# Rotary embedding of one attention: partner halves by four small SBUF copies in place of a rotation matmul, with TensorE's order rewritten

## The reference

```python
def apply_rope(t, cos, sin):
    tf = t.astype(jnp.float32)
    t1, t2 = tf[..., :HEAD_DIM // 2], tf[..., HEAD_DIM // 2:]
    return jnp.concatenate([t1 * cos - t2 * sin, t2 * cos + t1 * sin], axis=-1).astype(t.dtype)

def odd_mixer(h, w_in, w_out, cos, sin):
    q, k, v = jnp.split(h @ w_in, 3, axis=-1)
    o = moba_attention(apply_rope(to_heads(q, H_MOBA), cos, sin),
                       apply_rope(to_heads(k, H_MOBA), cos, sin),
                       to_heads(v, H_MOBA))
    return from_heads(o) @ w_out
```

## Time and profile before

| | |
|---|---|
| median of 3 runs | 1939.98 us (1939.98 to 1940.36) |
| the profiled execution, its own time | 1937.51 us |
| its span in the profile | 1935.7 us |
| TensorE busy | 1896.3 us, 98% of the span |
| DVE busy | 1391.6 us, 72% |
| ACT busy | 1024.7 us, 53% |
| the eight pairs, first Q to the third output slab | 406.58 to 489.50 us |

### The profile page before, as it was taken

How to read it: one execution, slowest core, us unless ns; L and a number is a source line. 1 busy time by engine, 2 the same in 40 slices (tenths; PEclk the granted TensorE clock), 3 DMA queues, 4 the chain that set the end, 5 groups by cost and what they waited for, 6 DMA issues and landing times.

```text
span 1935.7 us, 32388 instructions
## 1 busy us (share of the span) xinstructions
PE 1896.3 (98%) x11234; PEld 1638.0 (85%) x11234; DVE 1391.6 (72%) x2850; ACT 1024.7 (53%) x1739; POOL 335.9 (17%) x147
## 2 busy tenths in 40 slices
PE   8989999999999999999999999999999999999998
PEld 7867887788788889998899998888898988888886
DVE  6685556667655568898997678976778876666666
ACT  6565455555644466666434556665555553333333
POOL 0000000000000000000000268886666500000000
PEclk9999999999999999999999999999999999999999
DMA  6524655443355544443344445554444455555554
GB/s 222 195 77 134 217 182 173 143 153 120 131 186 187 190 141 156 149 135 110 131 138 165 145 144 183 185 186 152 142 142 142 141 185 194 191 191 193 195 194 153
DMA packets 85581, 314.11 MB, mean 162 GB/s; under 512 B 9504, under 2 KB 9632, under 8 KB 85280
## 3 DMA queue, kind: packets, MB, share of 16 engines
q1 hardware_dynamic: 85472, 312.65, 48.6%
HBM read 311.56 MB, written 1.05 MB: 161 GB/s over the span
## 4 chain that ended last, share of the span: by engine, by line
PE 87%; DVE 8%; ACT 3%; issue 1%; DMA 1%; SPq 0%; DVEq 0%; ACTq 0%
PE ps L416 23%; PE ps L401 13%; PE ps L2625 11%; PE ps L282 11%; PE ps L2629 6%; PE ps L1886 5%; PE ps L2809 3%; PE ps L2442 3%; PE ps L1955 2%; PE ps L788 1%; DVE wsplit L266 1%; PE ps L432 1%; DMA ring<-in_weights 1%; ACT wsplit L260 1%; PE ps L2271 1%
## 5 line engine op out<-in xcount | busy, mean ns | idle before, releaser
L260 ACT ACTIVATE wsplit<-ring 128x1024 fp32r<-128x1024 f32 x572 | 604.6, 1058 | 512.8 <-PE ps L416 266.4
L266 DVE TENSOR_TENSOR wsplit<-ring,wsplit 128x1024 fp32r<-128x1024 f32 x438 | 539.3, 1235 | 304.1 <-ACT wsplit L260 302.8
L416 PE MATMUL ps<-wsplit,gsplit 128*128 128x512 f32 x1992 | 456.5, 390 | 0.0
L266 POOL TENSOR_TENSOR wsplit<-ring,wsplit 128x1024 fp32r<-128x1024 f32 x134 | 321.7, 2402 | 696.3 <-ACT wsplit L260 696.0
L416 PEld LDWEIGHTS ps<-wsplit,gsplit 128*128 128x128 f32 x1992 | 373.2, 188 | 81.3 <-issue 4.0
L2625 PE MATMUL ps<-hsplit,wsplit 128*128 128x512 f32 x1024 | 368.3, 402 | 0.5 <-DVE work L2672 0.5
L401 PE MATMUL ps<-wsplit,hsplit 128*128 128x512 f32 x1248 | 299.7, 395 | 5.6 <-DVE wsplit L266 3.0
L2629 PE MATMUL ps<-hsplit,wsplit 128*128 128x256 f32 x1024 | 286.2, 280 | 0.0
L401 PEld LDWEIGHTS ps<-wsplit,hsplit 128*128 128x128 f32 x1248 | 232.7, 189 | 57.8 <-DVE wsplit L266 6.8
L282 PE MATMUL ps<-hsplit,wsplit 128*128 128x256 f32 x1992 | 258.5, 287 | 7.2 <-DVE hsplit L736 2.1
L282 PEld LDWEIGHTS ps<-hsplit,wsplit 128*128 128x128 f32 x1992 | 243.6, 191 | 17.4 <-issue 9.1
(11 more groups left out here) (325 smaller groups left out, 1945.5 us busy)
## 6 DMA issues: line engine op xcount, KB each, us to landing
ring<-in_weights SPq DMA_DIRECT2D x572, 512.0 KB, 3.3
work<-in_weights SPq DMA_DIRECT2D x8, 512.0 KB, 4.9
work<-in_tables SPq DMA_DIRECT2D x1, 1995.0 KB, 10.4
work<-in_decay SPq DMA_DIRECT2D x2, 512.0 KB, 4.0
work<-in_subkeys SPq DMA_DIRECT2D x2, 512.0 KB, 5.0
out_x<-work SPq DMA_DIRECT2D x2, 512.0 KB, 2.6
...
```

What stands on the lines that cost most here:

```text
L260: act.activation(wsplit[:, n % RING, 0, :], slab(s), ACT.Copy).then_inc(S("split", "lead"), 1)
L266: eng.tensor_tensor(wsplit[:, n % RING, 1, :], slab(s), wsplit[:, n % RING, 0, :], ALU.subtract).then_inc(S("split", RESTS[stream][0]), 1)
L416: mm = pe.matmul(YR[:, tt, half * 512:(half + 1) * 512], gsplit[:, slot, b, tt * P:(tt + 1) * P], wsplit[:, n, a, half * 512:(half + 1) * ...
```

## The change

The matmul with `rot` in this attention is gone. ACT copies query and key out of PSUM one by one, each as soon as its own product is done (`moba_raw_scalar`, L1222 of the changed kernel), waits for that copy, and issues four DMAs of 32 partitions x 256 elements (32 KB) from `qk_raw` to `qk_tmp`, which swap the halves of both heads: eight DMAs for each pair, 64 in all, from ACT's own queue. The sign of the rotation moves into the table `sin`, and `rot` loses its minus sign, since another attention goes on using both with instructions of the same kind and shape. `turn` is now called for query and key apart, with 128x256 operations. The copy for query u waits until both turns of pair u - 1 are done, the copy for key u until the turn of query u is done. TensorE's loop has the order Q(u+1), P(u-1), S(u), K(u+1), V(u-1), and the projections of pair 1 stand ahead of the loop.

```diff
--- before.py
+++ after.py
@@ -1139,18 +1139,24 @@
     def moba_pair(name, u):
         return S("pair", name), MOBA_FROM + u + 1
 
-    def moba_rotate_tensor(pe, st, u):
-        pe.wait_ge(*moba_pair("qk_sb", u))
-        pe.matmul(ps[:, 2, :], table("rot"), qk_raw[:, :, :].rearrange("p a t -> p (a t)"), start=True,
-                  stop=True).then_inc(S(st, "turned"), 1)
+    def moba_half(name, u, a):
+        return S("pair", name), MOBA_FROM + 2 * u + a + 1
 
     def moba_query_tensor(pe, st, u):
         if u:
-            pe.wait_ge(*moba_pair("qk_sb", u - 1))
-        split_project(pe, ps[:, 0, 0:T], st, 8 + 2 * u)
+            pe.wait_ge(*moba_half("qk_sb", u - 1, 0))
+        split_project(pe, ps[:, 0, 0:T], st, 8 + 2 * u).then_inc(S("pair", "qk"), 1)
 
     def moba_key_tensor(pe, st, u):
+        if u:
+            pe.wait_ge(*moba_half("qk_sb", u - 1, 1))
         split_project(pe, ps[:, 1, 0:T], st, 9 + 2 * u).then_inc(S("pair", "qk"), 1)
+
+    def moba_scores_tensor(pe, st, u):
+        pe.wait_ge(S(st, "qk_turn"), 2 * u + 2)
+        if u:
+            pe.wait_ge(*moba_pair("tops", u - 1))
+        scores_tensor(pe, qk_turn[:, 0, :], qk_turn[:, 1, :], 3).then_inc(S("pair", "scores"), 1)
 
     def moba_probs_tensor(pe, u):
         pe.wait_ge(*moba_pair("probs", u))
@@ -1179,26 +1185,21 @@
             mm.then_inc(S(st, "v"), 1)
         moba_query_tensor(pe, st, 0)
         moba_key_tensor(pe, st, 0)
-        moba_rotate_tensor(pe, st, 0)
-        for u in range(8):
-            last = u == 7
-            if not last:
-                moba_query_tensor(pe, st, u + 1)
-            pe.wait_ge(S(st, "qk_turn"), u + 1)
-            if u:
-                pe.wait_ge(*moba_pair("tops", u - 1))
-            scores_tensor(pe, qk_turn[:, 0, :], qk_turn[:, 1, :], 3).then_inc(S("pair", "scores"), 1)
-            if not last:
-                moba_key_tensor(pe, st, u + 1)
-            if u:
-                moba_probs_tensor(pe, u - 1)
-            if not last:
-                moba_rotate_tensor(pe, st, u + 1)
-            if u > 5:
-                pe.wait_ge(*moba_pair("o_low", u - 6))
-                out_tile_tensor(pe, "out1", u - 6, 0, hsplit, u == 6)
-            if u:
-                moba_values_tensor(pe, st, u - 1)
+        moba_query_tensor(pe, st, 1)
+        moba_key_tensor(pe, st, 1)
+        moba_scores_tensor(pe, st, 0)
+        for u in range(1, 7):
+            moba_query_tensor(pe, st, u + 1)
+            moba_probs_tensor(pe, u - 1)
+            moba_scores_tensor(pe, st, u)
+            moba_key_tensor(pe, st, u + 1)
+            moba_values_tensor(pe, st, u - 1)
+        moba_probs_tensor(pe, 6)
+        for c in range(2):
+            pe.wait_ge(*moba_pair("o_low", c))
+            out_tile_tensor(pe, "out1", c, 0, hsplit, c == 0)
+        moba_scores_tensor(pe, st, 7)
+        moba_values_tensor(pe, st, 6)
 
         def out(c):
             out_chunk_tensor(pe, "out1", c, hsplit, moba_pair("o_low", c))
@@ -1218,9 +1219,15 @@
     def moba_rest(v, k):
         rest_of(v, *(("moba", k) if k < N_MOBA else ("out1", k - N_MOBA)))
 
-    def moba_query_key_scalar(act, u):
-        act.wait_ge(*moba_pair("qk", u))
-        act.activation(qk_raw[:, :, :], ps[:, 0:2, 0:T], ACT.Copy).then_inc(S("pair", "qk_sb"), 1)
+    def moba_raw_scalar(act, st, a, u):
+        act.wait_ge(*moba_half("qk", u, a))
+        if u or a:
+            act.wait_ge(S(st, "qk_turn"), 2 * u + a)
+        act.activation(qk_raw[:, a, :], ps[:, a, 0:T], ACT.Copy).then_inc(S("pair", "qk_sb"), 1)
+        act.wait_ge(*moba_half("qk_sb", u, a))
+        for p in range(0, P, 64):
+            for to, at in ((p, p + 32), (p + 32, p)):
+                act.dma_start(qk_tmp[to:to + 32, a, :], qk_raw[at:at + 32, a, :]).then_inc(S(st, "turned"), 16)
 
     def moba_turned_scalar(act, u):
         act.wait_ge(*moba_pair("probsT", u))
@@ -1264,19 +1271,29 @@
         moba_lead(act, 10)
         values(1, 2)
         moba_lead(act, 11)
-        moba_query_key_scalar(act, 0)
+        moba_raw_scalar(act, st, 0, 0)
+        moba_raw_scalar(act, st, 1, 0)
         for u in range(8):
             last = u == 7
             if not last:
                 moba_lead(act, 12 + 2 * u)
-                moba_lead(act, 13 + 2 * u)
-                moba_query_key_scalar(act, u + 1)
-            if u > 5:
-                for c in (range(2), range(2, 6))[u - 6]:
-                    moba_split_scalar(act, c)
+                moba_raw_scalar(act, st, 0, u + 1)
+                if u == 0:
+                    moba_lead(act, 13)
+                    moba_raw_scalar(act, st, 1, 1)
             if u:
                 moba_turned_scalar(act, u - 1)
+            if u and not last:
+                moba_lead(act, 13 + 2 * u)
+            if last:
+                for c in range(2, 6):
+                    moba_split_scalar(act, c)
             moba_exps_scalar(act, u)
+            if u and not last:
+                moba_raw_scalar(act, st, 1, u + 1)
+            if u == 6:
+                moba_split_scalar(act, 0)
+                moba_split_scalar(act, 1)
             if u:
                 moba_out_scalar(act, u - 1)
         for k in range(26, 29):
@@ -1288,11 +1305,12 @@
         moba_lead(act, 31)
 
     def moba_vector(v, own, st):
-        def turn(u):
-            v.wait_ge(S(st, "turned"), u + 1)
-            own(v.tensor_tensor(qk_turn[:, :, :], qk_raw[:, :, :], cos_now, ALU.mult))
-            own(v.tensor_tensor(qk_tmp[:, :, :], ps[:, 2, :].rearrange("p (a t) -> p a t", a=2), sin_now, ALU.mult))
-            v.tensor_tensor(qk_turn[:, :, :], qk_turn[:, :, :], qk_tmp[:, :, :], ALU.add).then_inc(S(st, "qk_turn"), 1)
+        def turn(a, u):
+            v.wait_ge(*moba_half("qk_sb", u, a))
+            own(v.tensor_tensor(qk_turn[:, a, :], qk_raw[:, a, :], cos_now[:, a, :], ALU.mult))
+            v.wait_ge(S(st, "turned"), 64 * (2 * u + a + 1))
+            own(v.tensor_tensor(qk_tmp[:, a, :], qk_tmp[:, a, :], sin_now[:, a, :], ALU.mult))
+            v.tensor_tensor(qk_turn[:, a, :], qk_turn[:, a, :], qk_tmp[:, a, :], ALU.add).then_inc(S(st, "qk_turn"), 1)
 
         def probs(u):
             br = u % 2
@@ -1327,19 +1345,22 @@
         own(v.tensor_tensor(sin_now, sin2, by_token, ALU.mult))
         for k in range(7, 12):
             moba_rest(v, k)
-        turn(0)
-        for u in range(8):
+        turn(0, 0)
+        turn(1, 0)
+        for u in range(7):
+            moba_rest(v, 12 + 2 * u)
+            if u == 0:
+                moba_rest(v, 13)
+            tops(u)
+            turn(0, u + 1)
             if u:
-                probs(u - 1)
-            if u < 7:
-                moba_rest(v, 12 + 2 * u)
-            tops(u)
-            if u < 7:
                 moba_rest(v, 13 + 2 * u)
-                if u == 6:
-                    low(0)
-                    low(1)
-                turn(u + 1)
+            probs(u)
+            if u == 6:
+                low(0)
+                low(1)
+            turn(1, u + 1)
+        tops(7)
         for u in range(2, 7):
             low(u)
         probs(7)
@@ -3135,7 +3156,7 @@
     inv = (np.float32(10000.0) ** (-np.arange(0, HD, 2, dtype=np.float32) / np.float32(HD))).astype(np.float32)
     ang = np.arange(T, dtype=np.float32)[:, None] * inv[None, :]
     cos, sin = np.cos(ang.astype(np.float64)).T, np.sin(ang.astype(np.float64)).T
-    c4, s4 = np.tile(cos, (4, 1)), np.tile(sin, (4, 1))
+    c4, s4 = np.tile(cos, (4, 1)), np.concatenate([-sin, sin, -sin, sin], 0)
     q = HD ** -0.5
     t["cos"] = np.concatenate([c4 * q, c4], 1)
     t["sin"] = np.concatenate([s4 * q, s4], 1)
@@ -3143,7 +3164,7 @@
     rot = np.zeros((P, P))
     for h in range(2):
         for d in range(32):
-            rot[h * 64 + 32 + d, h * 64 + d] = -1.0
+            rot[h * 64 + 32 + d, h * 64 + d] = 1.0
             rot[h * 64 + d, h * 64 + 32 + d] = 1.0
     t["rot"] = rot
     causal = np.zeros((P, 384))
```

## The result

The changed kernel took **1976.3 us** (median of 4 runs, 1973.19 to 1981.52) against 1940.17 for the kernel before in the same runs (4 runs, 1939.98 to 1942.92): the ratio is **1.0192**, interval 1.018 to 1.0204. The forecast was 1952.3 with a range of 1941 to 1963. The side was right, the size was a third of what came: +36 us where +12.3 stood.

A forecast was written before the change was run, and what follows sets the result against it. TensorE was taken to bound the old kernel, and ACT's queue the new one. First scores +2.8, first to second scores +4.7, five middle pairs +2.1 and the end +2.7 summed to +12.3 us: median 1952.3, range 1941 to 1963.

The forecast's parts named there:

- a loop through ACT: Middle pairs: copies, issues, exponentials, landing and turn sum to 10.03 us a pair against 9.60 before; +2.1 us over five.
- wait for the turn ahead of the scores of pairs 2 to 6: TensorE has 8.5 us of work in a pair's loop and waits about 1.5 us ahead of each scores.
- longest ahead of the first transposes: TensorE waits 7.7 us for P(0), as pair 0's exponentials stand behind key 1's copy and issues on ACT.
- the later stages would neither give nor take: Stages behind the third output slab: every one unchanged in time.
- the price of an issue: ACT's queue: four DMA issues take 1.68 us, the fourth beginning at 1.23; bounds of one issue 0.05 and 0.45.
- the first scores: Head of the stage: key 0's copy waits for query 0's turn, so scores start at 419.9, not 417.10; +2.8 us.
- the second: From first to second scores: 13.3 us against 8.59, since the order costs most here; +4.7 us.
- the end: From the scores of pair 6 to the third output slab: 18.5 us against 15.8; +2.7 us.
- the landing: Time from the fourth issue's start until a small copy has landed: 2.0 us, with ends of 1.25 and 3.3.
- the copies wait out the ring loads: Rival, swap DMAs: landings of 3.3 us beside SP's loads, about +23 us in all, 1963; chance 0.10.
- the clock: Rival: the 7.7 us wait lowers TensorE's clock to 1.2 GHz, up to +4 us, 1956; chance 0.10.
- issues of 0.05 us: Rival: issues nearly free on ACT, so TensorE's 8.5 us binds a pair; -2.3 us, 1937.7; chance 0.12, 0.07 of it faster.

The follow-up runs named there:

- c1: Changed kernel with a completion semaphore each for query and key, relaxed copy guards, and the first pair ordered as the others; DMAs stay on ACT: 1953.95 us, ratio 1.0079.
- e1: Changed kernel with the swap DMAs issued by SP ahead of its ring load, relaxed guards and first pair ordered as the others: 1944.68 us, ratio 1.0027.
- a3: Changed kernel without the swap DMAs, the turn multiplying the half itself by sin, order of all engines kept: 1935.57 us, ratio 0.9986.
- f1: Changed kernel with one more wait on SP, so a ring load in the pairs is issued only after the swap under way has landed: 1971.35 us.
- b2: Changed kernel with unused 128x512 matmuls where TensorE waits, ahead of the first transposes and the scores of pairs 2 to 6: 1976.4 us, one run.

## Why the forecast was wrong

**Right.** That a pair would be bound by a loop through ACT, and its terms in their order; that busy time would not show it; that TensorE would wait for the turn ahead of the scores of pairs 2 to 6 (2.4 to 4.0 us, 1.5 forecast) and longest ahead of the first transposes (9.53 us, 7.7 forecast, put down to L920 as said); that the later stages would neither give nor take. c1, e1 and a3 bear the loop out: with wider guards, with these and the issues on SP ahead of the load, or without the DMAs the pair drops to 11.0 on average, and, after the first, to 9.2 to 9.5 and 8.45.

**The step that failed first: the price of an issue.** "The four stand in a row, so I take 0.33 + 3 x 0.45 = 1.68 us for four, the fourth beginning at 1.23." It is 2.44, the fourth beginning at 1.83. I took SP's loads, another form of DMA (ring loads for 0.33, two loads of other tiles in a row for 0.45), and called the latter the upper bound. That was no bound: the small copies inside SBUF take 0.61 from ACT and 0.59 from SP, the one of 128 partitions 0.47. The error was in the form of the DMA, not in the engine. In a pair it counts for 1.4 us, 7 in five pairs; 1.2 more come before the first scores (two times 0.6), 1.6 before the second and 1.6 at the end (two times 0.8 each): 11.4 of the 23.1 that are missing in the profiled executions (35.4 less 12.3).

**The second: the landing.** "I take 2.0, from the ring loads, since these run beside them." Alone it was 1.96, so the sum was right for a copy that has the engines to itself. But the rival "the copies wait out the ring loads" held: each half's swap meets a load, since both are released by the same turn, the copy at once, the load after the rest of a slab, 1.2 us. I weighed it by DMA's mean share of 36%, and a mean says nothing on two events that one cause starts together. f1, which took the load out of the swap's way, shows the collision. It is 1.2 us a pair, 6 in five, and 1.3 more in the last of them (4.48); the first landing of all took 4.2 us (fourth issue at 412.06, DVE at 416.27), another 2.2: 9.5. SP issues loads at that time, but no run tests this first one, and in f1 it still took 4.5. The longer landing also brought the path through the query's turn level with the loop, where the forecast left it 1.0 us of slack.

**The third, smaller: the clock.** It fell, as that rival said, but in the pairs it stands nowhere in the chain, and b2 gained nothing by raising it; about 1.6 us of it stand in the chain at the end, where nothing waits behind.

Together 11.4, 9.5 and 1.6 are 22.5. ACT copied query 0 at 409.76, 1.1 us earlier than I had placed it, since the whole stage began 1.0 us earlier, which goes the other way: 21.4. So 1.7 us stay with no step of their own.

**The range** ended at 1963, since it took one high price at a time (issues at 0.45 with a landing of 3.3). Both were high together, and the upper end of the issue was no end.

On the Trainium skill, "DMA: Bandwidth & Descriptors", section "Issuing engines are not separate DMA queues": that the time of the sequencer to start a DMA is usually small relative to the DMA itself does not hold here: 0.61 us for a DMA that lands in 1.96, and 2.44 for four. The case in which the rule would have decided, issues of 0.05 us, is out. The other thing that the section says, that DMAs issued from different engines run on the same DMA engines, agrees with this case: with the load delayed, the landing of ACT's copies fell from 3.2 to 1.9 us (medians).
